# Expert input products of 512 latent columns with a prompt product per four chunks, and late splits on ScalarE and VectorE

## The chip, the cores and the metric

The kernel runs on one core of one Trainium2 chip. The metric is the device time of one execution in microseconds (us).

## The reference, cut to what matters

Two trunk layers run over 128 prompt tokens and 512 latent tokens together (640 tokens, width 1024, all in float32). Each layer ends in a mixture of 16,384 experts that are chosen by product keys. This is the part that the change touches:

```python
def block(xb):                                   # h: 640 tokens, 1024 wide
    q = (xb @ wq).reshape(tb, 8, 2, 128)
    sc = jnp.einsum('thsd,hskd->thsk', q, subkeys)
    sv, si = lax.top_k(sc, 16)
    cand = (sv[:, :, 0, :, None] + sv[:, :, 1, None, :]).reshape(tb, 8, 256)
    best, ci = lax.top_k(cand, 16)
    idx = i1 * 128 + i2                          # 8 heads x 16 experts per token
    gsm = jax.nn.softmax(best, axis=-1)
    act = jax.nn.gelu(jnp.einsum('td,thkd->thk', xb, u_tab[idx]))
    return jnp.einsum('thk,thkd->td', gsm * act, v_tab[idx])
```

## The kernel before, in words

**Dense experts.** The kernel doesn't gather for the latent tokens. It multiplies all tokens by all 16,384 input rows (`u`), 128 experts at a time: 128 *chunks* per layer, each of 128 experts by 1024. For the 512 latent tokens it later multiplies the activations by a dense matrix of gates and that by all value rows (`v`), again in 128 chunks. For the 128 prompt tokens it gathers the 128 chosen activations and value rows per token with indirect DMAs.

**Precision.** Every product is made of three: high part by high part, low part of the tokens by high part of the weights, and high by low. A chunk that has landed in one of eight slots of `w_in` is *split*: a copy rounded to fp32r goes to `w_hi`, and the difference overwrites the chunk in place as `w_lo`. In the input stage GpSimd does both for every chunk (`split_loop`, L451 to L459, with `low` at L440); in the value stage ScalarE makes the high part (`high_v`, L1111) and VectorE the low one (`low_v`, L1561).

**The input stage** (`experts`). One chunk is 2 halves of 320 tokens x 8 slices of the width x 3 matmuls = 48 matmuls of 320 columns (`expert`, L693 to L705, with `linear_step` at L511, whose three matmuls are L515, L516 and L517). They go into one of two pairs of PSUM banks, `acc[0]` and `acc[1]`, in turn. ScalarE applies the gelu to all 640 tokens (L1046), counts `taken`, and stores the 512 latent columns to `act_s` (L1048) and the 128 prompt columns to `act_p` (L1050). SP loads a chunk into a slot as soon as the product that used the slot is `made` (`load_inputs`, L370). GpSimd waits for the load, splits, and counts `lo_done`, for which TensorE waits.

**Early and late chunks.** While the first 57 chunks run (7 x 8, and a `BRIDGE` of one), VectorE finds the chosen experts of all tokens (`route`). Then TensorE turns the picks (L719), and 64 *late* chunks follow, each with two gate groups between its matmuls (`late`, L734): for four tokens VectorE makes one-hot columns of the two keys (L1524, L1526), TensorE multiplies them in twelve small bf16 matmuls (`gates_of_four`, L723, matmul L730) into one of four halves of `aux`, and ScalarE copies that to one of two `gates` buffers (L1098). After eight groups, that is every four chunks, ScalarE issues two stores of 1 MB to `gate_s` (`store_gates`, L1081), whose rows are 32 tokens or 128 bytes long. Seven chunks without gates end the stage.

**Order.** Each engine runs its own list in order, written out by hand. On ScalarE in the late stage it is: activation and two stores of a chunk, two gate copies, and after the eighth copy the two gate stores. A DMA that ScalarE can't hand over holds up all that stands behind it there. On SP, loads of inputs are followed by the values' first loads and by the reloads of `act_s` and `gate_s`, which wait for the stores. On GpSimd the gathers for the prompt tokens come after the last split.

**Slots.** Chunk n of the whole program (weights of the other products are chunks too) goes to slot n % 8.

Of the kernel before, what the change touches and what calls it, by code (L numbers as in the profile page):

```python
# [4 lines left out]
P = 128  # L5
D, KD = 1024, 8
# [44 lines left out]

def chunk_at(layer, kind):
    return next(n for n, c in enumerate(CHUNKS) if c[0] == layer and c[1] == kind)
# [6 lines left out]
def build(nc, a):  # L60
# [3 lines left out]
    with ctx:  # L64
# [32 lines left out]
        iota_b = sb("iota_b", [P, P], BF)  # L97
        mask = sb("mask", [P, 384])
# [87 lines left out]
        where = at("where", [P, 2, PICKS], rope_at)  # L186
        where_i = at("where_i", [P, 2, PICKS], rope_at + 1024, U32)
        pick_act = at("pick_act", [P, PICKS], rope_at + 2048)
        part_now = at("part_now", [P, 8], rope_at + 2560)
        act_p = [nc.dram_tensor(f"act_p{l}", (NKEY * P * NP_TOK, 1), F, kind="Internal").ap() for l in range(2)]  # L190
        act_p_rows = [t.rearrange("(c p t) o -> c p (t o)", c=NKEY, p=P) for t in act_p]
# [42 lines left out]
        act_in = [sem(f"act_in{i}") for i in range(2)]  # L234
        part_ready, added, total_turned = sem("part_ready"), sem("added"), sem("total_turned")
# [12 lines left out]
        BRIDGE = 1  # L248
        BUILT = 2
# [10 lines left out]
        A_EARLY = EARLY * SPLIT // 2  # L260
        A_LATE = (NKEY - EARLY * SPLIT) // 4
# [3 lines left out]
        OCTETS = PICKS // 8  # L265
        GROUPS = NL_TOK // GROUP
# [37 lines left out]
        def split_by_pool(n):  # L304

            return n + 1 - NKEY * CHUNKS[n][0]
# [33 lines left out]
        def _(sp):  # L340
            def load_chunk(n):
                if n >= SPLIT:
                    sp.wait_ge(*last_use(n - SPLIT))
                sp.dma_start(landing(n % SPLIT, CHUNKS[n][3]), source(n)).then_inc(raw_in[n % SPLIT], 16)
# [12 lines left out]
            for l in range(2):  # L357
# [12 lines left out]
                def load_inputs(c, u):  # L370
                    slot = (UC[l] + u) % SPLIT
                    sp.wait_ge(made, UM[l] - SPLIT + 1 + c)
                    sp.dma_start(landing(slot), a["u"][l, bass.ds(c, 1)].rearrange("o p n -> (o p) n"))\
                      .then_inc(raw_in[slot], 16)

                if l == 0:
                    with sp.Fori(0, MODS_AT.start // SPLIT) as i:
                        for u in range(SPLIT):
                            load_inputs(u + SPLIT * i, u)
                    sp.wait_ge(shifted, 1)  # L380
                    for c in MODS_AT:
                        load_inputs(c, c % SPLIT)
# [4 lines left out]
                with sp.Fori(0 if l else MODS_AT.stop // SPLIT, BODIES) as i:  # L387
                    for u in range(SPLIT):
                        load_inputs(u + SPLIT * i, u)

                def load_values(c, u):
                    slot = (VC[l] + u) % SPLIT
# [10 lines left out]
                for u in range(GROUP):  # L403
                    sp.wait_ge(*last_use(VC[l] + u - SPLIT))
                    load_values(u, u)
                for k in range(2):
                    sp.wait_ge(gates_out[k], 16 * PIECES * 2 * (NT - 1) * (l + 1))
                for s in range(2):
                    sp.wait_ge(a_st[s], 32 * (A_ALL[s] * l + SPLIT // 2))
                for u in range(GROUP):  # L410
                    load_ag(u, u)
                for u in range(GROUP, SPLIT):
                    sp.wait_ge(*last_use(VC[l] + u - SPLIT))
                    load_values(u, u)
                for s in range(4):
                    sp.wait_ge(a_st[s], 32 * A_ALL[s] * (l + 1))
# [22 lines left out]
        def _(pool):  # L439
# [5 lines left out]
            def split_chunk(n):  # L445
                slot, size = n % SPLIT, CHUNKS[n][3]
                pool.wait_ge(raw_in[slot], 16 * (n // SPLIT + 1))
# [3 lines left out]
            def split_loop(l):  # L451
                first = UC[l]
                with pool.Fori(0, BODIES) as i:
                    for u in range(SPLIT):
                        n = first + u
                        pool.wait_ge(raw_in[n % SPLIT], 16 * (n // SPLIT + 1) + 16 * i)
                        pool.sem_inc(slot_ready, 1)
                        pool.tensor_copy(w_hi[:, n % SPLIT, :], landing(n % SPLIT)).then_inc(hi_done, 1)  # L458
                        low(split_by_pool(n) + SPLIT * i, n % SPLIT, 1024)  # L459
# [17 lines left out]
            def values_of(l):  # L477
# [5 lines left out]
                for s in range(4):  # L483
                    pool.wait_ge(a_st[s], 32 * A_ALL[s] * (l + 1))
# [18 lines left out]
        def _(pe):  # L503
            def begin(m):
# [4 lines left out]
                return acc[m % 2], PRODUCTS[m][4] % SPLIT  # L509
# [181 lines left out]
            def experts(l):  # L691

                def expert(m0, w, split_value, taken_value, beside=0, between=None):  # L693

                    pe.wait_ge(lo_done, split_value)
                    pe.wait_ge(taken[m0 % 2], taken_value)
                    spots = [2 * KD * (j + 1) // beside - 1 for j in range(beside)]
                    for h in range(2):
                        n = slice(h * HALF, (h + 1) * HALF)
                        for k in range(KD):  # L700
                            mm = linear_step(acc[m0 % 2][:, h, 0:HALF], w, P, k, KD, a_hi, a_lo, n)
                            if h == 1 and k == KD - 1:
                                mm.then_inc(made, 1)
                            if KD * h + k in spots:
                                between()  # L705

                with pe.Fori(0, EARLY) as i:
                    for u in range(SPLIT):
                        expert(UM[l] + u, (UC[l] + u) % SPLIT, split_by_pool(UC[l] + u) + SPLIT * i,
                               (UM[l] + u) // 2 + (SPLIT // 2) * i)  # L710
# [1134 lines left out]
```

## Time and profile before

| | us |
|---|---|
| median of 3 runs | 4620.28 |
| lowest and highest run | 4614.63, 4627.97 |
| the profiled execution | 4617.94 |
| its span from first to last instruction | 4616.1 |

The profile is of one execution. For each engine it gives busy time and, for idle time, what ended it. PE is TensorE's matmuls and PEld its weight loads, DVE is VectorE, ACT ScalarE, POOL GpSimd, SP SyncE; ACTq and SPq are those engines' sequencers, where DMA issues appear. Queue q10 holds ScalarE's DMAs, q1 those of SP. A name such as L1098 is a line of the kernel before. Matmuls overlap, so the time from one start to the next is what counts, not the duration of one. Layer 0's early input chunks run from 585 to 986 us, its late ones to 1605 us, and its values follow; layer 1's late ones run from 3273 to 3893 us.

### The profile page before, as it was taken

The numbers are of one execution on the slowest core, as the hardware profiler recorded it, in microseconds if no ns is written. First come the engines' busy times: TensorE is split into PE (matmuls) and PEld (weight loads), VectorE is DVE, ScalarE is ACT, GpSimd is POOL, SyncE is SP. The second block draws the span as 40 slices with busy tenths as digits, with TensorE's granted clock in tenths as the row PEclk, the third lists the DMA queues.
The fourth block names the chain that finished last, engine by engine and source line by source line (L and its number), as shares of the span: only waits on it lengthen the run. The fifth ranks groups of instructions, "written<-read, shape, count | busy, mean of one in ns | idle before, by whom it ended". The sixth has DMA issues, their size and how long they took to land.

```text
span 4616.1 us, 76065 instructions
## 1 busy us (share of the span) xinstructions
PE 4415.5 (96%) x27516; PEld 4019.7 (87%) x27516; DVE 3265.7 (71%) x6397; ACT 1197.8 (26%) x1696; POOL 1945.9 (42%) x1206
## 2 busy tenths in 40 slices
PE   7878999999999999999988889999999999999998
PEld 6857999999999988888886689999999999888887
DVE  6873199969999597877633432993599995766665
ACT  2043110022332233333233420101232332333332
POOL 2322455644444364444341134555444443544440
PEclk9978999999999999999998999999999999999999
DMA  5401234548777898888520012444477778888884
GB/s 202 161 19 46 67 112 125 181 118 165 161 153 159 218 354 312 312 314 309 204 74 23 24 60 67 119 125 118 117 159 163 158 152 241 321 287 294 288 287 141
DMA packets 823654, 797.70 MB, mean 173 GB/s; under 512 B 566513, under 2 KB 601041, under 8 KB 822898
## 3 DMA queue, kind: packets, MB, share of 16 engines
q1 hardware_dynamic: 175248, 500.38, 32.6%
q10 hardware_dynamic: 603106, 159.70, 16.1%
q0 software_dynamic: 45056, 134.38, 8.3%
q8 instruction: 152, 2.49, 0.2%
q14 instruction: 92, 0.75, 0.1%
HBM read 640.41 MB, written 153.89 MB: 172 GB/s over the span
## 4 chain that ended last, share of the span: by engine, by line
PE 82%; ACTq 8%; DVE 5%; ACT 3%; issue 2%; DMA 0%; DVEq 0%
PE acc L515 14%; PE acc L517 14%; PE acc L516 14%; PE aux L758 5%; PE acc L760 5%; PE acc L758 5%; PE aux L760 5%; PE aux L759 5%; PE acc L759 5%; ACTq L1048 4%; ACTq L1081 4%; PE aux L730 2%; PE aux L573 1%; ACT gates L1098 1%; PE aux L680 1%
## 5 line engine op out<-in xcount | busy, mean ns | idle before, releaser
L515 PE MATMUL acc<-a_hi,w_hi 128*128 128x320 f32 x5296 | 1673.5, 316 | 45.8 <-DVE a_lo L1288 32.9
L517 PE MATMUL acc<-a_hi,w_lo 128*128 128x320 f32 x5296 | 1643.8, 310 | 0.1
L516 PE MATMUL acc<-a_lo,w_hi 128*128 128x320 f32 x5296 | 1643.5, 310 | 0.0
L515 PEld LDWEIGHTS acc<-a_hi,w_hi 128*128 128x128 f32 x5296 | 1000.6, 189 | 50.9 <-issue 34.5
L516 PEld LDWEIGHTS acc<-a_lo,w_hi 128*128 128x128 f32 x5296 | 1000.9, 189 | 1.7 <-issue 0.5
L517 PEld LDWEIGHTS acc<-a_hi,w_lo 128*128 128x128 f32 x5296 | 999.0, 189 | 0.5 <-issue 0.3
L442 POOL TENSOR_TENSOR w_lo<-w_in,w_hi 128x1024 fp32r<-128x1024 f32 (+1 forms) x345 | 902.4, 2616 | 27.6
L458 POOL CAST w_hi<-w_in 128x1024 fp32r<-128x1024 f32 x256 | 311.3, 1216 | 1041.7 <-DMA w_in<-in_u 1041.7
L1526 DVE SCALAR_TENSOR_TENSOR one_b<-iota_b,picks_t 128x384 bf16<-128x384 bf16 x1024 | 632.9, 618 | 0.0
L1524 DVE TENSOR_SCALAR one_a<-iota_b,picks_t 128x128 bf16<-128x128 bf16 x1024 | 573.1, 560 | 60.0 <-PE aux L730 55.0
L467 POOL DMA_INDIRECT found<-in_v,where_i x256 | 315.3, 1231 | 509.1 <-DVE total L1586 401.7
L1565 DVE TENSOR_TENSOR w_lo<-w_in,w_hi 128x1024 fp32r<-128x1024 f32 x256 | 313.5, 1224 | 289.2 <-ACT w_hi L1114 288.2
L1046 ACT ACTIVATE a_out<-acc 128x640 f32<-128x640 f32 x184 | 129.9, 706 | 1157.5 <-PE acc L517 914.1
L473 POOL DMA_INDIRECT pick_act<-act_p,where_i x256 | 322.6, 1260 | 237.3 <-DVE part_now L1572 125.3
L448 POOL CAST w_hi<-w_in 128x1024 fp32r<-128x1024 f32 (+1 forms) x89 | 95.5, 1072 | 773.6 <-DMA w_in<-in_wq 333.4
L758 PE MATMUL aux<-p_his,w_hi 128*128 128x512 f32 x1024 | 399.1, 390 | 3.0 <-DVE p_los L1546 3.0
L758 PE MATMUL acc<-p_his,w_hi 128*128 128x512 f32 x1024 | 400.3, 391 | 0.0
L760 PE MATMUL acc<-p_his,w_lo 128*128 128x512 f32 x1024 | 399.1, 390 | 0.0
L759 PE MATMUL aux<-p_los,w_hi 128*128 128x512 f32 x1024 | 399.0, 390 | 0.0
L760 PE MATMUL aux<-p_his,w_lo 128*128 128x512 f32 x1024 | 399.0, 390 | 0.0
L759 PE MATMUL acc<-p_los,w_hi 128*128 128x512 f32 x1024 | 398.8, 389 | 0.0
L1098 ACT ACTIVATE gates<-aux 128x512 f32<-128x512 f32 x256 | 262.0, 1132 | 355.3 <-issue 325.6
(246 smaller groups left out, 5423.1 us busy)
## 6 DMA issues: line engine op xcount, KB each, us to landing
w_in<-in_u SPq DMA_DIRECT2D x256, 512.0 KB, 4.0
w_in<-in_v SPq DMA_DIRECT2D x256, 512.0 KB, 4.8
gate_s<-gates ACTq DMA_DIRECT2D x64, 1024.0 KB, 14.0
ag<-act_s SPq DMA_DIRECT2D x256, 256.0 KB, 5.0
ag<-gate_s SPq DMA_DIRECT2D x256, 256.0 KB, 6.1
act_s<-a_out ACTq DMA_DIRECT2D x184, 256.0 KB, 3.7
act_s<-tmp ACTq DMA_DIRECT2D x72, 256.0 KB, 3.6
w_in<-in_in SPq DMA_DIRECT2D x32, 512.0 KB, 4.6
```

The source lines that it names most:

```text
L442: pool.tensor_tensor(w_lo[:, slot, 0:size], landing(slot, size), w_hi[:, slot, 0:size].bitcast(F), ALU.subtract).then_inc(lo_done, 1)
L467: pool.indirect_dma_start(found[:, k % FOUND, :], None, rows_of_v, bass.IndirectOffsetOnAxis(ap=where_i[:, 0, k:k + 1], axis=0))\
L473: pool.indirect_dma_start(pick_act[:, k:k + 1], None, act_p[l], bass.IndirectOffsetOnAxis(ap=where_i[:, 1, k:k + 1], axis=0))\
L515: pe.matmul(out, wh, hi[:, k, n], start=(k == 0), stop=False)
L516: pe.matmul(out, wh, lo[:, k, n], start=False, stop=False)
L517: return pe.matmul(out, wl, hi[:, k, n], start=False, stop=(k == kt - 1))
L758: pe.matmul(v_bank(dt), wh, p_his[:, u, :], start=start, stop=False)
L759: pe.matmul(v_bank(dt), wh, p_los[:, u, :], start=False, stop=False)
L760: return pe.matmul(v_bank(dt), wl, p_his[:, u, :], start=False, stop=stop)
L1524: dve.tensor_scalar(one_a[:, tok % 8, :], iota_b[:], picks_t[:, 0, column], None, ALU.is_equal)
L1526: ins = dve.scalar_tensor_tensor(one_b[:, tok % 8], iota_b[:].unsqueeze(1).to_broadcast([P, 3, NKEY]), picks_t[:, 1, column], picks_t[:, 2 ...
L1565: dve.tensor_tensor(w_lo[:, slot, :], landing(slot), w_hi[:, slot, :].bitcast(F), ALU.subtract).then_inc(lo_v, 1)
```

## The change

A chunk's product now covers the 512 latent tokens alone: 8 x 3 matmuls of 512 columns into half of `acc[0]`. After four chunks one *prompt product* follows, with the 128 prompt tokens as the stationary side and the four chunks' slots as 512 moving columns: 8 x 3 matmuls into half of `acc[1]`. ScalarE's activation of a chunk has 512 columns and one store; the prompt activation (128 tokens by 512 experts) has its own buffer and one store in rows of 2 KB, and `act_p` is laid out by token. A slot is free again only when its group's prompt product is made, so the loads of four chunks wait for one count. The chunks are numbered so that inputs and values begin at slot 0 in both layers, and the slots of layer 1's first products follow from that. The early stage has 60 chunks (`BRIDGE` is four). From chunk 64 on, ScalarE makes the high part and VectorE the low part; GpSimd splits the first 64. The eight gate groups of four chunks come after every fifth of the 40 steps (a step is three matmuls), the last at the end of the prompt product. The index arithmetic for the gathers moves ahead of the softmax.

```diff
-        BRIDGE = 1
-        BUILT = 2
+        BRIDGE = GROUP
+        LATE = NKEY // 2
+        SPLIT_BOTH = NKEY - LATE + NKEY
...
+    start = {l: next(n for n, c in enumerate(CHUNKS) if c[:2] == (l, "u")) for l in range(2)}
+        w = (n - start[chunk[0]]) % SPLIT
...
+            if kind == "u":
+                return made_p, NKEY // GROUP * layer + i // GROUP + 1
...
+                def load_inputs(i, u):
+                    if isinstance(i, int) and i == 0:
+                        sp.wait_ge(*last_use(BEFORE[UC[l] + u]))
+                    else:
+                        sp.wait_ge(made_p, FOURS * l + u // GROUP - 1 + 2 * i)
+                    sp.dma_start(landing(u), a["u"][l, bass.ds(u + SPLIT * i, 1)].rearrange("o p n -> (o p) n"))\
+                      .then_inc(raw_in[u], 16)
...
-                with pool.Fori(0, BODIES) as i:
+                with pool.Fori(0, LATE // SPLIT) as i:
...
-                for s in range(4):
-                    pool.wait_ge(a_st[s], 32 * A_ALL[s] * (l + 1))
+                for k in range(2):
+                    pool.wait_ge(p_st[k], 16 * FOURS // 2 * (l + 1))
...
+                def latent_steps(m0, w, taken_value, split, split_value):
+                    pe.wait_ge(split, split_value)
+                    pe.wait_ge(taken[m0 % 2], taken_value)
+                    for k in range(KD):
+                        mm = linear_step(acc[0][:, m0 % 2, :], w, P, k, KD, a_hi, a_lo, slice(P, T))
+                        if k == KD - 1:
+                            mm.then_inc(made, 1)
+                        yield
+
+                def prompt_steps(g, first_slot, bank):
+                    if l or not (isinstance(g, int) and g < 2):
+                        pe.wait_ge(taken_p, FOURS * l + g - 1)
+                    w, n = slice(first_slot, first_slot + GROUP), slice(0, P)
+                    for k in range(KD):
+                        wh, wl = w_hi[:, w, k * P:(k + 1) * P], w_lo[:, w, k * P:(k + 1) * P]
+                        pe.matmul(acc[1][:, bank, :], a_hi[:, k, n], wh, start=(k == 0), stop=False)
+                        pe.matmul(acc[1][:, bank, :], a_lo[:, k, n], wh, start=False, stop=False)
+                        mm = pe.matmul(acc[1][:, bank, :], a_hi[:, k, n], wl, start=False, stop=(k == KD - 1))
...
+                        for _ in steps:
+                            done += 1
+                            if between is not None and done % 5 == 0:
+                                between(done // 5 - 1)
...
-                    act.activation(halves(out), feature(m0), ACT.Gelu_apprx_tanh).then_inc(taken[m0 % 2], 1)
+                    act.activation(out[:], acc[0][:, m0 % 2, :], ACT.Gelu_apprx_tanh).then_inc(taken[m0 % 2], 1)
...
-                    act.dma_start(act_p_rows[l][bass.ds(c, 1)].rearrange("o p n -> (o p) n"), out[:, 0:P])\
-                       .then_inc(a_st[slot], 16)
+                def prompt(g, k):
+                    act.wait_ge(made_p, FOURS * l + g + 1)
+                    if not (isinstance(g, int) and g < 2 and l == 0):
+                        act.wait_ge(p_st[k], 16 * (FOURS // 2) * l + 8 * (g - k))
+                    act.activation(p_out[k][:], acc[1][:, k, :], ACT.Gelu_apprx_tanh).then_inc(taken_p, 1)
+                    act.wait_ge(taken_p, FOURS * l + g + 1)
+                    act.dma_start(act_p_rows[l][:, bass.ds(4 * P * g, 4 * P)], p_out[k][:]).then_inc(p_st[k], 16)
...
+                def high_u(c, i):
+                    act.wait_ge(raw_in[c % SPLIT], 16 * LOADS[UC[l] + c] + 32 * i)
+                    act.activation(w_hi[:, c % SPLIT, :], landing(c % SPLIT), ACT.Copy).then_inc(hi_v, 1)
...
+                        take_gates(i, g, 0)
+                        take_chunk(0)
+                        take_gates(i, g, 1)
+                        take_gates(i, g, 2)
+                        take_chunk(1)
+                        take_gates(i, g, 3)
+                        high_u(first + GROUP, i)
+                        take_chunk(2)
+                        take_gates(i, g, 4)
+                        high_u(first + GROUP + 1, i)
+                        take_gates(i, g, 5)
+                        high_u(first + GROUP + 2, i)
+                        take_chunk(3)
+                        high_u(first + GROUP + 3, i)
+                        take_gates(i, g, 6)
+                        prompt(first // GROUP + 4 * i, first // GROUP % 2)
+                        take_gates(i, g, 7)
...
+                        for j in ((), (0,), (1,), (2, 3))[max(0, q % 8 - 4)]:
+                            low_u(LATE + GROUP * (q // 8) + j, i)
+
+                def low_u(c, i):
+                    dve.wait_ge(hi_v, input_by_both(l, c) + 4 * GROUP * i)
+                    dve.tensor_tensor(w_lo[:, c % SPLIT, :], landing(c % SPLIT), w_hi[:, c % SPLIT, :].bitcast(F),
+                                      ALU.subtract).then_inc(lo_v, 1)
```

## Rows read from the trace of the kernel before

**Rows 1.** The page's busy times: busy us (share of the span) xinstructions
```profile
PE 4415.5 (96%) x27516; PEld 4019.7 (87%) x27516; DVE 3265.7 (71%) x6397; ACT 1197.8 (26%) x1696; POOL 1945.9 (42%) x1206
```

**Rows 2.** Windows: from:to, length, busy of PE, PEld, DVE, ACT, POOL; clock, DMA share, GB/s
```profile
585.20:986.20 401.00, 401.00 (x2737) 401.00 (x2736) 352.11 (x1097) 42.90 (x59) 225.53 (x114) 1.00 0.47 141
986.20:1605.20 619.00, 601.00 (x4958) 584.47 (x4957) 539.03 (x1034) 185.06 (x216) 261.24 (x137) 1.00 0.73 164
1800.00:1900.00 100.00, 100.00 (x443) 82.84 (x442) 80.56 (x105) 30.87 (x38) 42.25 (x35) 1.00 0.89 316
2331.00:2345.00 14.00, 13.58 (x58) 10.26 (x57) 5.96 (x8) 8.97 (x13) 0.00 (x0) 1.00 0.00 0
3273.00:3893.00 620.00, 601.41 (x4958) 584.68 (x4957) 533.78 (x1034) 184.83 (x216) 264.12 (x137) 1.00 0.72 163
```

**Rows 3.** Timeline of PE in the late stage: the gate products alone
```profile
1103.09 0.84 PE L730 MATMUL aux<-one_b,one_a 128*128 128x128 bf16 x12
1107.35 0.84 PE L730 MATMUL aux<-one_b,one_a 128*128 128x128 bf16 x12
```

**Rows 4.** Waits of PE in the late stage of layer 0
```profile
PE aux L730 <- ACT gates L1098: 6.2, 9, 1.1
```

**Rows 5.** Timeline of DVE in the late stage, one-hots of one side
```profile
1103.30 0.24 DVE L1524 TENSOR_SCALAR one_a<-iota_b,picks_t 128x128 bf16<-128x128 bf16 x1
1103.99 1.03 DVE L1524 TENSOR_SCALAR one_a<-iota_b,picks_t 128x128 bf16<-128x128 bf16 x1
1105.47 2.39 DVE L1524 TENSOR_SCALAR one_a<-iota_b,picks_t 128x128 bf16<-128x128 bf16 x1
```

**Rows 6.** Timeline of POOL beside it
```profile
1105.04 2.76 POOL L442 TENSOR_TENSOR w_lo<-w_in,w_hi 128x1024 fp32r<-128x1024 f32 x1
```

**Rows 7.** Timeline of ACT in layer 0's late stage: gate stores and what follows
```profile
1034.57 7.68 ACTq L1081 DMA_DIRECT2D gate_s<-gates  x2
1043.09 6.77 ACTq L1048 DMA_DIRECT2D act_s<-a_out  x1
...
1206.89 7.40 ACTq L1081 DMA_DIRECT2D gate_s<-gates  x2
1214.46 0.71 ACT L1046 ACTIVATE a_out<-acc 128x640 f32<-128x640 f32 x1 [7.72 <-issue]
1215.35 7.70 ACTq L1048 DMA_DIRECT2D act_s<-a_out  x1
...
1223.74 1.93 ACT L1098 ACTIVATE gates<-aux 128x512 f32<-128x512 f32 x2 [8.58 <-issue]
1225.45 0.76 ACT L1046 ACTIVATE tmp<-acc 128x640 f32<-128x640 f32 x1
...
1559.26 7.88 ACTq L1081 DMA_DIRECT2D gate_s<-gates  x2
...
1568.10 6.98 ACTq L1048 DMA_DIRECT2D act_s<-a_out  x1
```

**Rows 8.** Timeline of DVE after the turned picks of layer 0
```profile
990.34 0.43 DVE L1512 CAST part_b<-picks_t 128x512 bf16<-128x512 f32 x1 [37.53 <-ACT picks_t L1076]
```

**Rows 9.** Groups by line in layer 0's late stage, the first value chunks' splits
```profile
L1114 ACT ACTIVATE w_hi<-w_in 128x1024 fp32r<-128x1024 f32 x5 | 5.3, 1060 | 5.1 <-ACT tmp L1046 1.8 <-ACT a_out L1046 1.8 <-DMA w_in<-in_v 1.5
L1565 DVE TENSOR_TENSOR w_lo<-w_in,w_hi 128x1024 fp32r<-128x1024 f32 x3 | 3.7, 1225 | 31.8 <-ACT w_hi L1114 31.8
```

**Rows 10.** DMA from 1219.95 to 1223 us: all packets, the one load issued
```profile
DMA packets 3580, 0.46 MB, mean 150 GB/s; under 512 B 3580, under 2 KB 3580, under 8 KB 3580
w_in<-in_u SPq DMA_DIRECT2D x1, 512.0 KB, 6.0
```

**Rows 11.** DMA from 1216 to 1217 us by queue: packets, MB, share
```profile
q1 hardware_dynamic: 102, 0.40, 98.3%
q10 hardware_dynamic: 78, 0.01, 6.2%
```

**Rows 12.** Timeline of PE: the first product of layer 1
```profile
2325.75 0.77 PE L558 MATMUL acc<-w_hi,a_hi 128*128 128x512 f32 x1 [12.65 <-DVE a_lo L1288]
```

More of the change, by code:

```diff
@@ L49, with slots @@
 CHUNKS, PRODUCTS = plan()
+def slots():
+    slot, before, loads, had = [], [], [], {}
+    start = {l: next(n for n, c in enumerate(CHUNKS) if c[:2] == (l, "u")) for l in range(2)}
+    for n, chunk in enumerate(CHUNKS):
+        w = (n - start[chunk[0]]) % SPLIT
+        last, count = had.get(w, (None, 0))
+        slot.append(w)
+        before.append(last)
+        loads.append(count + 1)
+        had[w] = n, count + 1
+    return slot, before, loads
+SLOT, BEFORE, LOADS = slots()
 def chunk_at(layer, kind):
@@ L707, in experts @@
[L707 to L710, printed above, removed]
-                for c in range(SPLIT * EARLY, SPLIT * EARLY + BRIDGE):
-                    expert(UM[l] + c, (UC[l] + c) % SPLIT, split_by_pool(UC[l] + c), (UM[l] + c) // 2)
+                    for k in range(KD):
[3 more added lines that the diff above has]
+                        yield
@@ new lines, in four_chunks @@
+                def four_chunks(c, i, far, split, split_value, between=None):
+                    done = 0
+                    for j in range(GROUP + 1):
+                        if j < GROUP:
+                            m0 = UM[l] + c + j
+                            steps = latent_steps(m0, (c + j) % SPLIT, m0 // 2 + far // 2 * i, split,
+                                                 split_value(c + j) + far * i)
+                        else:
+                            steps = prompt_steps(c // GROUP + far // GROUP * i, c % SPLIT, c // GROUP % 2)
+                        for _ in steps:
+                            done += 1
+                            if between is not None and done % 5 == 0:
+                                between(done // 5 - 1)
@@ new lines, in by_pool, with by_both, early @@
+                def by_pool(c):
+                    return split_by_pool(UC[l] + c)
+                def by_both(c):
+                    return input_by_both(l, c)
+                def early(i):
+                    for c in (0, GROUP):
+                        four_chunks(c, i, SPLIT, lo_done, by_pool)
+                for m in (UM[l] - 2, UM[l] - 1):
+                    has_taken(pe, m)
+                early(0)
+                with pe.Fori(1, EARLY) as i:
+                    early(i)
+                four_chunks(EARLY * SPLIT, 0, 0, lo_done, by_pool)
@@ L774, in values @@
                                     has_taken(pe, m)
+                            if first and u == 0 and dt == 6:
+                                pe.wait_ge(taken_p, FOURS * (l + 1))
                             mm = value_step(dt, u, first and u == 0, False)
```

211 lines of the change are left out of this document (105 added, 106 removed).

## The prediction

> **What bounds the kernel now.** I read the page's busy times first: TensorE is busy for most of the span [rows 1]. Then I cut the two layers into stages and read each alone [rows 2]. In the first stage of the expert inputs (57 chunks) TensorE has no idle time at all, in the value stage neither; in the late input stage, where gates are built beside the products, 18 of some 620 us are idle in either layer. So the time is the number of matmuls times the step of one, plus what the late stage loses.
>
> The step: 401.0 us over 57 x 48 products of 320 columns is 146.6 ns; 100 us over 443 products of 512 columns is 225.7 ns [rows 2]. At the granted clock of 1.00 (2.4 GHz) the columns alone take 133.3 and 213.3 ns, so each product carries 12 to 13 ns beside them.
>
> The late stage: two groups of gates (twelve bf16 products each) lie 4.26 us apart with 24 products between [rows 3]; less 24 x 0.1466 = 3.52, a group costs 0.74. TensorE's own work for four chunks is 192 x 0.1466 + 8 x 0.74 = 34.06 us, but the gate stores come every 34.98 us ((1559.26 - 1034.57) / 15) [rows 7]. About 0.9 us per four chunks is waiting; the largest named part is for ScalarE's copies of the gates [rows 4]. Two causes can be seen. VectorE makes a pair of one-hots in 0.69 us, but the one that meets a GpSimd split takes 1.03 or 2.39 us instead of 0.24 [rows 5] (the split beside it [rows 6]). And ScalarE stands in its own DMA issues: from the issue of the first gate store to the point where the next activation store is taken pass 15.29, 16.16 and 15.82 us [rows 7]. Over layer 0's sixteen such blocks it is 15.3 to 16.4, mean 15.9. I call this block B.
>
> **The change, part by part.**
>
> *Products.* Four chunks cost 192 products of 320 columns before, and 96 + 24 = 120 of 512 after: the same columns, 72 instructions fewer. 192 x 0.1466 = 28.14 us becomes 120 x 0.2257 = 27.09: 1.05 us per four chunks, 67 us over 64 groups, if nothing waits. The prompt product streams its weights from four slots at once. The trace has that form in layer 1's first products, where 58 take 13.6 us, 0.23 each [rows 2], so I charge nothing.
>
> The Trainium skill, page "TensorE: Matmul & The Clock Gate", section "Back-to-back issue gap", gives the isolated gap at full clock as columns / 2.4 plus 2.5 ns. By that, 72 fewer would save 0.18 us per group and 11.5 us in all. Here the trace disagrees: 12 to 13 ns beside the columns, not 2.5 [rows 2].
>
> *Early stage.* 60 chunks are early instead of 57: 15 x 27.09 = 406.3 us for 401.0. A slot is now freed only by its group's prompt product, so four loads come at once. With two groups of slots 27 us remain for them: some 5 us of DMA (below) and four splits on GpSimd at 4.0 us each (225.5 us busy for 57 chunks [rows 2]), together 21. Nothing waits. Routing was ready 37.5 us before TensorE asked [rows 8]; arriving 5 us later costs nothing, and the index arithmetic that moves ahead of the softmax on VectorE lies in that slack.
>
> *Late stage, VectorE and GpSimd.* GpSimd no longer splits here, so the collisions go. VectorE gets four low parts at 1.23 [rows 9]: 32 x 0.69 + 4.9 = 27 us for four chunks, under TensorE's 27.09 + 8 x 0.74 = 33.0. It has 6 us to spare.
>
> *Late stage, ScalarE.* Per group it gains four casts at 1.06 [rows 9] and a prompt activation with its store, and loses four small stores (0.5 each). It works in order, and B lies in that order. Time 0 is TensorE's end of the eighth gate group. ScalarE first does the prompt activation (0.6, an estimate from 0.71 for 640 columns [rows 7]), a semaphore (0.2) and the issue (0.5), then the eighth copy (1.05); the gate store is issued at 1.9. During B it manages one copy and the next group's first activation. Then come two copies (1.7 [rows 7]) and the second activation (0.6, with 0.3 of latency), at B + 4.5. TensorE's fourth chunk needs the bank that this frees. Unhindered it would start at 24 x 0.677 + 4 x 0.74 = 19.2; from there 13.8 us remain to the group's end. So the period is P = max(33.0, B + 18.3). ScalarE's work outside B is 16.5, 1.8 us under that, so the casts end within the group and no low part is late.
>
> *What B becomes.* An input load that is issued while a gate store is being issued does not start: after 1219.95 only packets under 512 B move for 3 us, and it lands after 6.0 us [rows 10]. When it gets its turn, the stores stand: 102 of its 4 KB packets in one microsecond leave 78 of theirs [rows 11]. So loads and gate stores take turns, and each load in a block costs it time. Loads come every 8.7 us, so one or two fall in a block; I read the 15.3 as one and the 16.2 as two, 0.9 each (a load's 128 packets take 1.26). After the change none comes during the block. But the prompt product's end, at -0.74, releases four: SP issues them from -0.6 to about 1.5, and at 0.9 each they are done at 3.2, so the store issued at 1.9 waits 1.3. Without loads B would be 15.3 - 0.9 = 14.4; with 1.3 it is 15.7, and their last packets hinder the first gate packets a little: I take 15.9, as now, and P = 34.2. Bounds: 14.4 if the burst is quite over (P = 33.0); below, nothing is to be had. Above, all of the burst's packets lie inside the block, 512 / 102 = 5.0 us: 19.4 (P = 37.7). I stay near the lower end, since the burst is released 2.6 us ahead of the store.
>
> *Ends of the stages.* The late stage before is 16 x 34.98 + 7 x 7.035 + 10.1 (turning the picks and the first gates' wait, unchanged). After: 406.3 + 10.1 + 16 P + four chunks without gates 27.1 = 443.5 + 16 P, against 401.0 + 619.0 = 1020.0. The values' first four loads still have that 27 us; the next four come at the stage's end and have four value chunks (21.7 us). In layer 1 the slots shift by one, so one chunk of the first products loads only after the last value product; TensorE waits 12.65 us for VectorE there anyway [rows 12]. No cost. Prompt stores in 2 KB rows replace 512-byte ones off the path.
>
> **Sum.** P = 34.2 gives 990.7, 29.3 us less per layer, 59 us for both. The profiled execution took 4617.9 us (span 4616.1); 4559 results, and the median of the runs shown is 2.3 above that execution: 4562 us. A measurement of this kernel can tell about 0.3% (14 us) from no change. The break-even is P = 36.0, B = 17.7.
>
> **Rivals.**
> - *The burst is over before the store* (B under 15.3). For it: the loads are issued first, and a free block has no load in it. P = 33.0 gives 443.5 + 528 = 971.5, 97 us off: 4523; P = 33.6 gives 4542. Chance 0.22.
> - *The burst blocks ScalarE* (B over 17.3): the gate packets nearly stop under loads [rows 11], ScalarE stands in its DMA issue, and TensorE at its fourth chunk. From B = 17.7 it is slower; at 18.5, P = 36.8, 1032.3: 25 us more for both layers, 4645; at 19.4, 53 us more, 4673. Against it: the blocks of now lose under 1 us per load. Chance 0.18, of which 0.08 within 0.3% and 0.10 slower.
> - *The casts come late*: if the 1.8 us of slack on ScalarE are too few, low parts hold TensorE at a group's first chunk; 3 us per group is 96 us: 4658. Chance 0.05.
> - *The prompt product does not do what it says*, its four slabs costing a fixed part each: 3 x 12.4 ns x 24 x 64 = 57 us back, 4619, no change; against it, [rows 2]. Chance 0.03.
> - *Forecast*, B 15.3 to 17.3, P 33.6 to 35.6: 4542 to 4606. Chance 0.52.
>
> Faster: 0.52 + 0.22 = 0.74; same 0.08 + 0.03 = 0.11; slower 0.10 + 0.05 = 0.15. The range, 4525 to 4630, leaves out the floor of the first rival and the slower half of the second and the third.
>
> **What would show it.** Right: early chunks at 6.77 us without idle; late waits of PE only at a group's fourth chunk, released by ScalarE's activation; one-hots at 0.24 throughout the late stage; gate stores 34.2 us apart, B 15.9. Wrong: PE waiting for low parts, gate stores over 36 us apart, or steps of the prompt product over 0.23 us.

## The result, and the profile after

The changed kernel takes 4644.44 us (median of 5 runs, 4640.08 to 4649.36) against 4620.28 us (5 runs, 4609.73 to 4627.97): a ratio of 1.0055, 95% interval 1.0037 to 1.0073. It is slower, by 24 us, where 4562 us and a gain were forecast. The profiled execution took 4645.27 us (span 4643.5).

The page shows less work and more time. Its first line, and the shares by line of the chain that ended last, which is the work followed back from the last instruction:

```profile
PE 4380.5 (94%) x22908; PEld 3638.5 (78%) x22908; DVE 3076.7 (66%) x6525; ACT 1327.8 (29%) x1888; POOL 1421.2 (31%) x950
...
PE acc L555 11%; PE acc L557 11%; PE acc L556 11%; ACTq L1166 5%; PE aux L831 5%; PE aux L833 5%; PE aux L832 5%; PE acc L831 5%; PE acc L832 5%; PE acc L833 5%; ACTq L1123 3%; PE acc L750 3%; PE acc L752 2%; PE acc L751 2%; PE aux L805 2%
```

TensorE executes 4608 products fewer than in [rows 1], exactly 72 x 64, and is busy 35 us less. In the chain stand L1166 and L1123, ScalarE's issues of the gate store and of the activation store: a DMA's issue, not its landing, lies on the path. They are not new there. The page of the kernel before has the same two issues, as L1081 and L1048, in the same part of its chain:

```profile
PE acc L515 14%; PE acc L517 14%; PE acc L516 14%; PE aux L758 5%; PE acc L760 5%; PE acc L758 5%; PE aux L760 5%; PE aux L759 5%; PE acc L759 5%; ACTq L1048 4%; ACTq L1081 4%; PE aux L730 2%; PE aux L573 1%; ACT gates L1098 1%; PE aux L680 1%
```

Windows of the stages (columns as in [rows 2]): early chunks, late stage, and layer 1's late stage, which runs from the turning of its picks at 3293.2 us to its last input product at 3920.3:

```profile
581.10:989.20 408.10, 408.10 (x1803) 337.98 (x1802) 349.87 (x1098) 47.76 (x78) 213.09 (x114) 1.00 0.39 141
989.20:1612.80 623.60, 574.21 (x3589) 455.71 (x3587) 442.23 (x1098) 245.00 (x293) 7.30 (x7) 0.99 0.68 152
3293.20:3920.30 627.10, 581.38 (x3589) 461.45 (x3587) 442.18 (x1098) 245.40 (x293) 7.91 (x8) 0.98 0.67 151
```

The early stage has no idle time and takes 408.1 us where 406.3 were forecast. Nearly the whole miss is in the second window: 623.6 us instead of 584.4, with 49 us of idle TensorE where [rows 2] had 18. What it waits for, in the waits of TensorE over layer 0's late stage (total us, times, longest):

```profile
PE acc L555 <- ACT l_out L1121: 42.2, 32, 2.2
PE aux L831 <- DVE p_los L1663: 4.9, 2, 3.4
PE acc L555 <- issue: 3.3, 2, 1.8
```

The waits for the copies of the gates [rows 4] are gone; in their place 32 waits stand for ScalarE's activations, two a group, at the third and at the fourth chunk, where a bank of `acc` is to be freed. Why ScalarE is late is in its timeline (start, length, instruction; a DMA's length is that of its issue):

```profile
1180.40 10.24 ACTq L1166 DMA_DIRECT2D gate_s<-gates  x2
1190.80 1.09 ACT L1180 ACTIVATE gates<-aux 128x512 f32<-128x512 f32 x1 [10.58 <-issue]
1191.70 0.62 ACT L1121 ACTIVATE l_out<-acc 128x512 f32<-128x512 f32 x1
1192.50 5.76 ACTq L1123 DMA_DIRECT2D act_s<-l_out  x1
1198.37 1.91 ACT L1180 ACTIVATE gates<-aux 128x512 f32<-128x512 f32 x2 [6.05 <-issue]
1200.08 0.62 ACT L1121 ACTIVATE l_out<-acc 128x512 f32<-128x512 f32 x1
...
1215.16 0.34 ACTq L1133 DMA_DIRECT2D act_p<-p_out  x1
...
1216.90 10.19 ACTq L1166 DMA_DIRECT2D gate_s<-gates  x2
...
1228.97 5.07 ACTq L1123 DMA_DIRECT2D act_s<-l_out  x1
```

The block that the prediction calls B, from the first gate store's issue to the point where the next activation store is taken, is 1192.50 + 5.76 - 1180.40 = 17.86 us. Over the 32 blocks of both layers it is 17.1 to 19.2, mean 18.10; before it was 15.9 in layer 0. The two issues of the gate store take 10.2 us here where [rows 7] has 7.4 to 7.9. Two groups lie 36.50 us apart in these rows; over layer 0 it is (1583.29 - 1031.87) / 15 = 36.76, forecast 34.2. The layer's stages then take 443.5 + 16 x 36.76 = 1031.7 us, which is what the first two windows add up to, and 11.7 more than before: 23.4 us for two layers, of the 24 measured.

Stage by stage the two profiled executions, whose spans are 27.4 us apart, say much the same. From the first input chunk to the first value product the changed kernel is 11.6 us longer in layer 0; from the last value product of layer 0 to the first of layer 1 it is 13.3 longer; layer 0's values add 6.5; and what lies ahead of the first input chunk is 4.1 us shorter.

What lies in front of the store is in SyncE's timeline:

```profile
1214.46 2.22 SPq L411 DMA_DIRECT2D w_in<-in_u  x4
```

And in the DMA of that block by queue (packets, MB, share; q1 is SyncE's, q10 ScalarE's), from 1217 to 1222 us and then from 1223 to 1228:

```profile
q1 hardware_dynamic: 440, 1.61, 84.7%
q10 hardware_dynamic: 288, 0.28, 16.0%
```

```profile
q10 hardware_dynamic: 7066, 0.90, 156.4%
```

The four loads are issued at 1214.46, the gate store at 1216.90. In the five microseconds that follow, 440 packets on the loads' queue move and 288 on ScalarE's, and of all these only 208 are under 512 B; then 7066 such packets move in the same time. Of the 512 packets of the four loads the first starts at 1215.4 and 500 have started by 1222.1, and the gate store's 16384 begin in earnest at 1222: 5.1 us after its issue.

### The profile page after: what moved, and what is told of

Read it like the earlier page. It is cut to its first block, busy times and chain, and to the rows that moved or that the text cites. A ratio compares the mean times of both kernels' runs of the same rounds, so it can differ in the third digit from the quotient of the medians.

```text
span 4643.5 us, 66396 instructions
## 1 busy us (share of the span) xinstructions
PE 4380.5 (94%) x22908; PEld 3638.5 (78%) x22908; DVE 3076.7 (66%) x6525; ACT 1327.8 (29%) x1888; POOL 1421.2 (31%) x950
## 4 chain that ended last, share of the span: by engine, by line
PE 80%; ACTq 9%; DVE 5%; ACT 3%; issue 2%; DMA 1%; DVEq 0%; SPq 0%
PE acc L555 11%; PE acc L557 11%; PE acc L556 11%; ACTq L1166 5%; PE aux L831 5%; PE aux L833 5%; PE aux L832 5%; PE acc L831 5%; PE acc L832 5%; PE acc L833 5%; ACTq L1123 3%; PE acc L750 3%; PE acc L752 2%; PE acc L751 2%; PE aux L805 2%
## 5 line engine op out<-in xcount | busy, mean ns | idle before, releaser
L555 PE MATMUL acc<-a_hi,w_hi 128*128 128x512 f32 (+1 forms) x3248 | 1210.9, 373 | 122.6 <-ACT l_out L1121 80.4
L557 PE MATMUL acc<-a_hi,w_lo 128*128 128x512 f32 (+1 forms) x3248 | 1177.3, 362 | 0.0
L556 PE MATMUL acc<-a_lo,w_hi 128*128 128x512 f32 (+1 forms) x3248 | 1177.2, 362 | 0.0
L555 PEld LDWEIGHTS acc<-a_hi,w_hi 128*128 128x128 f32 x3248 | 617.0, 190 | 223.7 <-issue 99.1
L557 PEld LDWEIGHTS acc<-a_hi,w_lo 128*128 128x128 f32 x3248 | 616.2, 190 | 82.5
L556 PEld LDWEIGHTS acc<-a_lo,w_hi 128*128 128x128 f32 x3248 | 618.1, 190 | 72.7 <-issue 0.5
L482 POOL TENSOR_TENSOR w_lo<-w_in,w_hi 128x1024 fp32r<-128x1024 f32 (+1 forms) x217 | 535.8, 2469 | 17.4
L1633 DVE TENSOR_SCALAR one_a<-iota_b,picks_t 128x128 bf16<-128x128 bf16 x1024 | 257.5, 251 | 195.0 <-PE aux L805 192.6
L1223 ACT ACTIVATE w_hi<-w_in 128x1024 fp32r<-128x1024 f32 x256 | 270.0, 1056 | 270.6 <-DMA w_in<-in_v 267.5
L1703 DVE SCALAR_TENSOR_TENSOR total<-found,part_now,total 128x1024 f32<-128x1024 f32 x254 | 326.4, 1285 | 11.0 <-DVE part_now L1689 9.8
```

The costliest lines, as they stand in the source:

```text
L482: pool.tensor_tensor(w_lo[:, slot, 0:size], landing(slot, size), w_hi[:, slot, 0:size].bitcast(F), ALU.subtract).then_inc(lo_done, 1)
L555: pe.matmul(out, wh, hi[:, k, n], start=(k == 0), stop=False)
L556: pe.matmul(out, wh, lo[:, k, n], start=False, stop=False)
L557: return pe.matmul(out, wl, hi[:, k, n], start=False, stop=(k == kt - 1))
L1703: dve.scalar_tensor_tensor(total[:], found[:, u, :], part_now[:, u:u + 1], total[:], ALU.mult, ALU.add).then_inc(added, 1)
```

## The experiments

Two numbers are read where the argument needs them: B (mean over the blocks of both layers) and P, the mean distance of layer 0's gate stores. Time is the median of the runs; ratios are against the kernel before on the same chip.

**1. The stores on another engine.** SyncE issues each gate store behind the group's four loads.

```
+ store_gates(1, 16 * i - 128, P + 64 * i - 544)   # SyncE, behind loads 0 to 3
+ store_gates(0, 16 * i - 120, P + 64 * i - 512)   # SyncE, behind loads 4 to 7
- if q == 7: ... store_gates(g % 2, piece, ...)    # ScalarE
```

> The changed kernel, with the gate stores issued by SyncE behind each group's four loads, so that ScalarE never stands in one. Theory (the block): TensorE's late waits for ScalarE's activation and copies go, the gate groups come 33.0 to 33.4 us apart instead of 36.76, which over 32 groups is 108 to 120 us less than the changed kernel: 4524 to 4540 us. Rival 1 (the order of ScalarE's own work, casts included, is what is late): the period stays above 34.5, the time above 4570. Rival 2 (the store's traffic as such holds everything up, whoever issues it): the loads behind a store come late on SyncE's queue, TensorE waits for low parts, and the time stays above 4600.

4543.65 us (4537.98 to 4544.70, ratio 0.9834, 0.9813 to 0.9856): 101 us under the changed kernel, and P 33.6 (33.2 within a loop body, 34.9 and more where the loop over groups turns). Both lie just above the theory's ranges and below those of either rival. SyncE's timeline, and all the waits that TensorE has left from 1040 to 1580 us:

```profile
1189.70 2.19 SPq L411 DMA_DIRECT2D w_in<-in_u  x4
1192.18 10.91 SPq L431 DMA_DIRECT2D gate_s<-gates  x2
```

```profile
PE acc L573 <- issue: 3.3, 2, 1.8
PE aux L849 <- DVE p_los L1677: 1.5, 1, 1.5
```

The issue still takes 11 us, behind the same burst; but now an engine stands in it that nobody waits on. ScalarE's casts are all still there and no wait on them is left, which rejects rival 1; the traffic is the same, which rejects rival 2. The Trainium skill, page "DMA: Bandwidth & Descriptors", section "Issuing engines are not separate DMA queues", says that issuing from several engines saves only the sequencer's time to issue, usually small beside the transfer. The first half is what this run shows; here that time was not small, 10 us of each 37 on the engine that frees the banks.

**2. The burst behind the block.** The stores stay on ScalarE; each late burst is released by the second gate copy of the next group.

```
- sp.wait_ge(made_p, FOURS * l + u // GROUP - 1 + 2 * i)     # u = 4 of body 8; from body 9 on, u = 0 and 4
+ sp.wait_ge(gate_read, GROUPS * l + {0: 16 * i - 126, 4: 16 * i - 118}[u])
```

> The changed kernel, with each late burst of four loads released by ScalarE's second gate copy of the next group, which lies behind the block, instead of by the prompt product's end, which lies ahead of it. Theory (the burst lengthens the block): B falls from 18.1 to 14.4 to 15.0, as for a block without loads, the period to 33.0 to 33.6, the time to 4524 to 4545 us. Rival (the prompt activation's store with 2 KB rows, which ScalarE issues just ahead, or the store by itself is what has become longer): B stays at 17.5 to 18.5 and the time within 15 us of 4644. Rival (the loads then come too late for the casts): B falls, but TensorE waits for low parts and the period is 34 to 36, the time 4555 to 4620.

4552.34 us (ratio 0.9856, 0.9834 to 0.9878); B 15.0 (14.6 to 15.3, mean 14.85, and over 17 only in the last block of either layer, where the first value loads are not moved), P 33.75. Time and P are a little above the theory's range (4545, 33.6), but no wait for a low part of the inputs stands in TensorE's list, so the second rival is not the reason. ScalarE's timeline, and the DMA from 1195 to 1200 us:

```profile
1191.80 0.34 ACTq L1140 DMA_DIRECT2D act_p<-p_out  x1
...
1193.54 7.43 ACTq L1173 DMA_DIRECT2D gate_s<-gates  x2
...
1202.90 5.25 ACTq L1130 DMA_DIRECT2D act_s<-l_out  x1
```

```profile
q10 hardware_dynamic: 5667, 0.73, 92.2%
```

Nothing but the place of the four loads has moved, and the store's issue is back at 7.4 us and its packets move at once. The prompt store still goes ahead of it and is not the cause.

**3. Half of the burst.** Two loads as in the changed kernel, two as in experiment 2.

```
+ {2: 16 * i - 126, GROUP + 2: 16 * i - 118}.get(u)   # the wait on gate_read at the third load
```

> The changed kernel, with two loads of each late burst released by the prompt product's end as they are, and two only by ScalarE's second gate copy of the next group, behind the block. Theory (the store's packets wait until the burst's have moved): two loads and the prompt store are through about 2 us after the store's issue instead of 5.2, so most of the extra goes with half of the loads: B 15.0 to 16.0, the period 33.3 to 34.3, the time 4545 to 4580 us. Rival (each load in front costs the same, a quarter of the 3.1 us between 15.0 and 18.1): B 16.3 to 16.8, the period 34.6 to 35.1, the time 4585 to 4605. Rival (one load in front is enough): B over 17.5, the time over 4620.

4574.46 us (ratio 0.9898, 0.9883 to 0.9914); B 16.0, P 34.68. Two of four loads leave 1.0 of the 3.1 us. B and the time lie in the theory's ranges, at their upper ends; P lies in those of the first rival. So the run shows that half of the burst costs less than the whole, and does not tell well whether it costs a third or a half. The five microseconds that begin 0.1 us after a store's issue (1207.34), by queue as above:

```profile
q10 hardware_dynamic: 3587, 0.70, 75.2%
q1 hardware_dynamic: 183, 0.62, 39.3%
```

183 packets of the loads' queue are left to move where the changed kernel has 440, and the store's come in numbers from 1210, 2.7 us after its issue.

**4. The prompt's store taken off ScalarE**, issued by SyncE behind the loads.

```
- act.dma_start(act_p_rows[l][:, bass.ds(4 * P * g, 4 * P)], p_out[k][:])
+ sp.dma_start(act_p_rows[l][:, bass.ds(4 * P * g, 4 * P)], p_out[k][:])   # behind each group's loads
```

> The changed kernel, with the late prompt activations' stores (2 KB rows) issued by SyncE behind the loads instead of by ScalarE just ahead of the gate store. Theory (the burst): B stays at 17.7 to 18.5, the period at 36.2 to 37, the time at 4630 to 4650 us. Rival (the prompt store on ScalarE's queue is what holds the gate store up): B falls to 16.5 or less, the period to 34.8 or less, the time to 4585 us or less.

4664.91 us (ratio 1.0098, 1.0074 to 1.0122); B 19.4, P 37.47. The rival is rejected, but B rose by 1.3 instead of staying, and time and P left the theory's ranges. The trace suggests why: ScalarE, free of one issue, reaches the gate store earlier against the burst, which now has a fifth transfer at its end. At 1176.71 the store is issued, and its packets come in numbers only from 1183.5, 6.8 us later instead of 5.1. Of the two changes, no run tells which counts for how much.

These four kernels and the changed one give B and P as

```
kernel            B      B + 18.3   P measured   time us
experiment 2     15.0      33.3       33.75      4552.34
experiment 3     16.0      34.3       34.68      4574.46
changed          18.1      36.4       36.76      4644.44
experiment 4     19.4      37.7       37.47      4664.91
```

The prediction's formula P = max(33.0, B + 18.3) holds within 0.5 us for these four. Its floor is low: with next to no store P is 33.53 (experiment 9), so experiment 2 lies on the floor and does not test B + 18.3. Over the other three P rises by 2.8 us while B rises by 3.4. Experiments 5 and 7, where other waits decide, do not belong on this line.

**5. The splits given back to GpSimd** in the late stage, as before the change: no casts on ScalarE, no low parts on VectorE.

```
- LATE = NKEY // 2
+ LATE = NKEY
- high_u(first + GROUP, i)   # and the three others, and VectorE's low_u
```

> The changed kernel with the split of the late chunks given back to GpSimd: no casts on ScalarE and no low parts on VectorE in the late input stage. Theory (the block): ScalarE's casts lie behind the place that TensorE waits for, so B stays at 17.7 to 18.5 and the period at 36 to 37: 4620 to 4650 us. One-hots that meet GpSimd take 1 to 2.4 us again, which the longer period hides. Rival (the casts made ScalarE late): the period falls to 34.5 or less and the time to 4575 us or less.

4777.29 us (ratio 1.0337, 1.0313 to 1.0361): neither. B is 18.1 as the theory had it, so the casts don't lengthen it, but P is 40.6. TensorE's waits from 1040 to 1580 us, GpSimd's timeline and the one-hots beside it:

```profile
PE aux L805 <- DVE one_b L1631: 60.1, 13, 5.1
```

```profile
1207.84 1.04 POOL L498 CAST w_hi<-w_in 128x1024 fp32r<-128x1024 f32 x1 [26.00 <-DMA w_in<-in_u]
1208.96 2.40 POOL L482 TENSOR_TENSOR w_lo<-w_in,w_hi 128x1024 fp32r<-128x1024 f32 x1
...
1220.15 2.54 POOL L482 TENSOR_TENSOR w_lo<-w_in,w_hi 128x1024 fp32r<-128x1024 f32 x1
```

```profile
1213.16 2.38 DVE L1629 TENSOR_SCALAR one_a<-iota_b,picks_t 128x128 bf16<-128x128 bf16 x1
1215.46 1.42 DVE L1631 SCALAR_TENSOR_TENSOR one_b<-iota_b,picks_t 128x384 bf16<-128x384 bf16 x1
1216.81 2.33 DVE L1629 TENSOR_SCALAR one_a<-iota_b,picks_t 128x128 bf16<-128x128 bf16 x1
```

Four loads that land together are split together: from 1207.84 to 1222.7 GpSimd works without a pause, and a pair of one-hots takes 3.6 us instead of 0.7. In the kernel before, GpSimd mostly paused for 3 to 7 us between two splits, and the same collisions [rows 5, 6] cost little. With loads in bursts, moving the split off GpSimd is not a refinement but a condition.

**6. The kernel before with its stores on SyncE**, to price the block there.

```
+ if u == 0: store_gates(1, 16 * i - 128, P + 64 * i - 544)       # SyncE, between single loads
+ if u == GROUP: store_gates(0, 16 * i - 120, P + 64 * i - 512)
```

> The kernel before, with its gate stores issued by SyncE between the loads instead of by ScalarE. Theory: TensorE's own work for four chunks is 34.06 us, with some 0.2 at loop ends as in the changed kernel, against 34.98 measured; part of that is ScalarE's block, part VectorE's collisions with GpSimd. If the block is most of it, the period is 34.2 to 34.5 and the time 4600 to 4610 us; the rest of the change (fewer, wider products, the split moved) is then worth the 55 to 65 us between this and the 4544 of the changed kernel with the same stores. Rival (the collisions are all of it): the period stays at 34.8 to 35.1, 4615 to 4625.

4724.50 us (ratio 1.0232, 1.0214 to 1.0250): neither, and of no use for the price. The timelines of SyncE and GpSimd, and TensorE's wait:

```profile
1176.27 7.34 SPq L391 DMA_DIRECT2D gate_s<-gates  x2
1183.88 8.30 SPq L373 DMA_DIRECT2D w_in<-in_u  x1
```

```profile
1197.36 1.04 POOL L477 CAST w_hi<-w_in 128x1024 fp32r<-128x1024 f32 x1 [17.51 <-DMA w_in<-in_u]
...
1205.97 2.54 POOL L461 TENSOR_TENSOR w_lo<-w_in,w_hi 128x1024 fp32r<-128x1024 f32 x1
```

```profile
1209.14 1.46 PE L749 MATMUL aux<-one_b,one_a 128*128 128x128 bf16 x12 [3.66 <-DVE one_b L1543]
```

SyncE issues in order, and the load behind a store takes 8.3 us to be issued instead of 0.33; its packets start at 1193.5, and until 1193 nearly all that moves on SyncE's queue is the store's own. So loads that came every 8.7 us land bunched behind a store, three splits run in a row, and TensorE waits for the one-hots as in experiment 5. What cured the changed kernel harms the kernel before.

**7. The gates all among the latent products**, one group every four steps: the third part of the change undone. The store then comes ahead of the burst.

```
- if between is not None and done % 5 == 0: between(done // 5 - 1)
+ if between is not None and done % 4 == 0 and done <= 32: between(done // 4 - 1)
```

> The changed kernel, with the eight gate groups of four chunks all among the latent products, one every four steps, and none in the prompt product; ScalarE's order follows. The gate store is then issued 5.4 us earlier against the prompt product's end, about 3.5 us ahead of the burst of loads. Theory (packets of loads and store share the engines): the burst lies inside the block and its 6.6 us of packets are added to it, B 19 to 21; as the block begins 5.4 us earlier in the group, the place that TensorE waits for moves little: period 35 to 38, time 4590 to 4685 us. Rival (only what lies ahead of the store delays it): B 14.5 to 15.5, the period 33.0 to 34.0, the time 4524 to 4560.

4741.87 us (ratio 1.0256, 1.0239 to 1.0272). B is 21.2 and P 39.6; like the time they lie above the theory's ranges. The rival is rejected; the theory has the direction and not the size. ScalarE's timeline of one group, and two windows of it:

```profile
1189.32 9.28 ACTq L1166 DMA_DIRECT2D gate_s<-gates  x2
1198.79 0.60 ACT L1131 ACTIVATE p_out<-acc 128x512 f32<-128x512 f32 x1 [9.64 <-issue]
1199.56 7.89 ACTq L1133 DMA_DIRECT2D act_p<-p_out  x1
```

```profile
1205.00:1210.00 5.00, 1.73 (x16) 1.44 (x16) 3.26 (x9) 1.74 (x3) 0.00 (x0) 0.98 1.33 172
1210.00:1213.00 3.00, 3.00 (x8) 2.30 (x7) 0.00 (x0) 2.37 (x4) 0.00 (x0) 0.50 0.24 91
```

The prompt's store now stands in the block, until 1199.56 + 7.89 - 1189.32 = 18.1 us after its beginning, and only then comes the next group's first activation. The expectation left out that the prompt's store stands behind the gate store on the same engine. TensorE is idle for 3.3 us, and its clock is then at 0.50 for three more (after most groups of this run for longer), which no term had either.

**8 and 9. Both kernels with next to no store**: only the first key of each half is written, and the value stage reads the activations twice.

```
- keys = slice(NKEY // PIECES * piece, NKEY // PIECES * (piece + 1))
+ keys = slice(NKEY // PIECES * piece, NKEY // PIECES * piece + 1)
```

> The kernel before, with each gate store cut to the first key of its half (128 rows of 128 B instead of 8192), so that no block stands in ScalarE's order and nothing is moved to another queue. Left out: most of the gates never reach memory, and the value stage reads the activations a second time in their place, by loads of the same size. Theory: what the late stage loses to ScalarE's block is at most 34.98 less TensorE's own 34.06 and some 0.3 at loop ends, 0.6 per four chunks: 4592 to 4605 us. Rival (the collisions of VectorE and GpSimd are the whole loss): 4612 to 4625.

> The changed kernel with the same cut: 128 rows per gate store, and the activations read twice in the value stage. Left out: most of the gates never reach memory. Theory: with no block the late groups take what TensorE needs, 33.2 and some 0.3 at loop ends, as where SyncE issued the stores: 4530 to 4550 us. Against the kernel before with the same cut it should then be 55 to 70 us faster, which is the forecast of 1.05 us per four chunks over 64 groups (67 us) less three added early chunks. Rival (a part of the change costs something that has nothing to do with the stores): the difference is under 45 us.

The kernel before takes 4599.67 us so (ratio 0.9954, 0.9940 to 0.9967), the changed one 4534.09 us (0.9811, 0.9795 to 0.9828). TensorE's waits from 1040 to 1580 us, of the one and of the other:

```profile
PE acc L515 <- issue: 4.2, 2, 2.2
```

```profile
PE acc L555 <- issue: 3.7, 2, 1.9
PE aux L831 <- DVE p_los L1663: 1.5, 1, 1.5
```

Both are at what TensorE needs. In the first P is 34.61, 34.0 to 34.1 in most groups and 37.9 and more where the loop turns; in the second it is 33.53. Without the stores the change is worth 4599.7 - 4534.1 = 65.6 us by the medians.

With them the changed kernel pays 4644.4 - 4534.1 = 110 us, and its trace has that where the theory puts it: from the turning of the picks to the first value product, layer 0 takes 625.1 us against 572.4 in experiment 9, layer 1 628.6 against 572.8. Those two differences are 108.5.

The kernel before pays 22 us by the medians (4622.0 - 4599.7), but only half of it is seen at the stores. Between the two profiled executions 11 us lie in the two late stages, 0.37 per four chunks (34.98 - 34.61), and 10 lie ahead of the first input chunk, where no gate is stored yet: from 230 to 380 us the granted clock was 0.73 in the kernel before and 0.83 in experiment 8. Whether that belongs to the edit or to the execution is not shown. So the block cost the kernel before between 11 and 22 us.

The traffic of the stores is left out here with the block. Experiment 1 moves all of it and is 9.6 us above experiment 9, most of which is one wait of 8.7 us at the first value chunks of layer 0; so the block alone is about 100 of the 110.

## Why the prediction was wrong

It came out as the second rival, *the burst blocks ScalarE*, which had a chance of 0.18 (0.10 for slower). The mechanism was in the prediction, the path and the wait too; what failed is a size. The step that failed is one term in "What B becomes": "at 0.9 each they are done at 3.2, so the store issued at 1.9 waits 1.3".

- *The rate of the burst.* 0.9 us was read as the difference between a block with one load in it and one with two [rows 7]. The trace has no such pair: in each of the first fifteen blocks of layer 0 the packets of one load move, 128 to 135 of 4 KB, in the block of 15.3 at 1034.57 (128) as in that of 16.2 at 1206.89 (132). Why these two differ is not shown. One load inside a block does cost about that much, 15.9 against 14.85 without any in experiment 2 (another kernel, so this is rough), and the figure was near by luck; but it is not what each of four takes in a row. 500 of the 512 packets took 6.7 us, some 1.7 a load, and held the store for 5.1 us behind its issue, not 1.3. The row that prices it was at hand: 102 packets in a microsecond [rows 11] (98 of them of 4 KB, by its 0.40 MB) are 5.0 us for 512, and I used it only for the upper bound. The prompt's own store, which goes out during the burst, was not counted at all.
- *What that does to B.* Not all of the 5.1 us reaches it. A block without loads is 14.85, not 14.4, and the burst adds 3.25 to it, not the 1.5 that I charged: 18.1 in all where I had 15.9.
- *P from B* was right in its size, within 0.5 us over four kernels, and so was the break-even: B of 17.7 was named as the point from which it is slower, and 18.1 made it slower. P came out 2.56 us over the forecast, 2.2 from B and 0.36 from the formula; on each of 32 groups that is 82, the distance from 4562 to 4644. The waits were named for the fourth chunk alone, and stand at the third too.
- *Why the lower end drew me.* "The burst is released 2.6 us ahead of the store" weighs issue against issue. What counts is when the last packet has moved, and a lead of 2.6 us does not cover 6.7 us of packets.
- *Products*: 1.05 us per four chunks, 67 us in all; 65.6 measured between experiments 8 and 9, and 34.61 - 33.53 = 1.08 by their P. The prompt product's four slabs cost nothing extra, as the early stage's 408.1 us show.
- *Casts and collisions*: right. One-hots of one side average 251 ns over the kernel, no wait for a low part is left, and the casts don't touch B. That the collisions cost the kernel before part of its 0.9 us was wrong: with the stores cut it has no wait of that kind left between 1040 and 1580 us. Of the 0.92 between 34.06 and 34.98 the stores make 0.37, and 0.55 is left without them, which stands where the loop turns.
- *Ends of the stages*: the first product of layer 1 waits 12.47 us for VectorE, as in [rows 12]. The first value chunks wait 4.9 us for VectorE in layer 0 (1.5 before), which the sum left out; with it layer 0's values take 707.6 us from the first product to the last instead of 701.1.

*What stays open*: the packets show that the store's come behind the burst's, but not why: whether the DMA engines serve what came first, or the making of the store's addresses is held up. No run separates these two.

The best of the kernels run is that of experiment 1: the change with the gate stores on SyncE, 4543.65 us, 1.7% faster than the kernel before. Ahead of it only the two ACTq lines in the chain pointed that way, and they stood in the page before the change already.

## What to carry to other kernels

When a change gathers transfers that were spread, price the burst by its packets in a row (their number over the packets that a row shows in a microsecond) and by its end, and ask who issues a DMA behind it: that engine may stand still, as ScalarE did here, whatever its own work. Gathered loads also gather whatever is done to each on landing; a collision that is harmless once in 9 us can stop the kernel when four follow each other. A long issue belongs on an engine on which nobody waits, but only if nothing that is spaced on purpose stands behind it there, as experiments 1 and 6 show with opposite signs.

## What the runs showed of the hardware that I had not expected

- The length of a DMA's issue depends on what other transfers are under way: the same two gate stores were taken in 7.4 to 8.1 us with no load ahead (experiment 2), 8.0 to 10.2 with two (experiment 3), 10.2 to 12.1 with four (the changed kernel), and in experiment 6 one plain load behind a store took SyncE 8.3 us to issue where it takes 0.33 otherwise. The Trainium skill, page "Perfetto Trace Analysis", section "What 'DMA-bound' means", reads such a slice on the issuing engine as the making of descriptors, not the moving of data. Here the descriptors of the store were the same and the slice grew with the loads ahead of it, so its length is not set by their number alone.
- A short idle stretch of TensorE can cost more than it lasts. In experiment 5 it stood 4.58 us and then worked at a granted clock of 0.50, its lower level of 1.2 GHz. TensorE's timeline there, and two windows (columns as in [rows 2]):

```profile
1215.57 0.39 PE L557 MATMUL acc<-a_hi,w_lo 128*128 128x512 f32 x1
1220.54 1.46 PE L805 MATMUL aux<-one_b,one_a 128*128 128x128 bf16 x12 [4.58 <-DVE one_b L1631]
1221.76 0.78 PE L555 MATMUL acc<-a_hi,w_hi 128*128 128x512 f32 x1
```

```profile
1220.00:1222.00 2.00, 1.46 (x13) 1.46 (x14) 2.00 (x2) 0.00 (x0) 1.92 (x2) 0.50 0.95 146
1222.00:1224.00 2.00, 2.00 (x8) 1.57 (x8) 2.00 (x5) 0.41 (x1) 0.69 (x1) 0.67 0.92 144
```

The gate group takes 1.46 us instead of 0.84, and the first product 0.78. From 1220.54 to about 1223.3 TensorE works at half the clock, which is some 1.4 us lost (an estimate from the two windows). Over 1100 to 1500 us the clock is 0.93 there and 1.00 in the changed kernel.

The changed kernel is not free of it. In its layer 1 six waits for an activation, of 1.8 to 2.6 us, were followed by a stretch at 0.50, while others of nearly 2 us were not. One of the six lasted 2.57 us and ended at 3682.1; these are the three microseconds up to there and the three behind it:

```profile
3679.00:3682.00 3.00, 0.54 (x3) 0.10 (x1) 2.80 (x8) 1.40 (x2) 0.00 (x0) 0.94 0.55 74
3682.00:3685.00 3.00, 2.89 (x7) 2.31 (x8) 0.00 (x0) 0.06 (x1) 0.00 (x0) 0.50 0.96 147
```

In layer 0 the same befell one of the 32 waits. Layer 1's late stage takes 627.1 us where layer 0's takes 623.6. So the late stage's losses are not linear: most of the changed kernel's waits of about 1.3 us cost what they last, those of experiments 5 and 7 more.
